# Expert stage of a hybrid diffusion step: rows gathered and added back by indirect DMA, weights in longer rows, an unrolled order

## The chip, the cores and the metric

One core of a Trainium2 chip runs the whole kernel. The metric is the device time of one execution in microseconds, the median of the runs shown. TensorE (PE) multiplies, VectorE (DVE) and ScalarE (ACT) work on tiles in SBUF and PSUM, GpSimd (POOL) does small work and issues some DMAs, SyncE (SP) issues the weight loads.

## The reference

One inference step of two layers on 128 context tokens and 256 latent tokens of 1024 channels. Layer 0 is differential attention and a dense SwiGLU, layer 1 a Fourier mixing and a top-2-of-8 expert SwiGLU; all is float32. The part that changes is the experts of layer 1:

```python
def moe_swiglu(h, w_router, w_gu_e, w_down_e):
    hf = h.reshape(-1, D_MODEL)
    probs = jax.nn.softmax((hf @ w_router).astype(F32), axis=-1)
    topv, topi = lax.top_k(probs, TOP_K)
    topv = topv / jnp.sum(topv, axis=-1, keepdims=True)
    gates = jnp.sum(jax.nn.one_hot(topi, N_EXPERTS) * topv[..., None], axis=1)
    out = jnp.zeros(hf.shape, F32)
    for e in range(N_EXPERTS):
        out = out + gates[:, e:e + 1] * swiglu(hf, w_gu_e[e], w_down_e[e])
    return out.reshape(shp)
# swiglu(h, w_gu, w_down): g, u = split(h @ w_gu); (silu(g) * u) @ w_down
# D_MODEL 1024, D_FF 2816, so w_gu_e[e] is 1024 x 5632 and w_down_e[e] 2816 x 1024
```

## The kernel before

All 384 tokens are handled together, as three tiles of 128. Every weight matrix is streamed from HBM in units of 1 MB (128 partitions x 2048 floats) into six slots `raw`. To multiply float32 accurately, each unit is split in two: ScalarE copies it to `ring_hi` in the type that TensorE multiplies fast (line 772 in the expert stage), VectorE subtracts to get the rest, `ring_lo` (line 1185). There are three such split slots (`RING`). The tokens are split in the same way. `mm3` (lines 1360 to 1364) does three matmuls for one product: high by high, low by high, high by low.

Each engine has its own program; semaphores order them. `unit_used` counts units that TensorE has finished, `hi_ready` and `lo_ready` the splits. SyncE loads unit m into a raw slot once unit m-6 has its low part; ScalarE splits a unit once its ring slot is used; both run two units ahead of TensorE (`AHEAD`).

The expert stage handles one expert at a time, with at most 128 of its tokens in the common path; a further block, which runs only where an expert has more than 128 tokens, stands behind it (its branch isn't taken with these inputs). A loop runs four times over a pair of experts. An expert has 33 units: 11 chunks of 256 gate and 256 up columns, each chunk two units (`gu`, half of the 1024 rows each, rows of 256 floats in HBM), and 11 `down` units of 256 rows. The order is gu, gu, then the down unit of the chunk before, so that TensorE has a down unit to do while ScalarE takes tanh and VectorE forms the hidden product `eh` (lines 1278 and 1281). `eh` is turned by TensorE (line 1694), split (lines 820 and 1268) and used by the down unit. Two PSUM banks take turns for gate/up, banks 4 and 5 collect the down product, 6 and 7 serve the rest.

The tokens of an expert are gathered by a product with a 0/1 matrix `sel`, which VectorE makes by comparing positions (line 1237): `gather_rows` (line 1645) multiplies `sel` by the split tokens `tok_hi` and `tok_lo`, 12 matmuls of 512 columns, `turn_gathered` (line 1654) turns the result into `xe`. After the expert its result `y`, split in two (lines 835 and 1285), is brought back to token order by the product with the turned selection (`bring_back`, line 1668, 12 matmuls of 512 columns), scaled by the gate and added to `acc` by VectorE (line 1261). These pieces are set by hand between the units of the next expert:

```python
COMBINE_AT = (8, 11, 14, 17, 18, 20)
NEXT_SEL_AT = 21
ROWS_AT = (24, 27)
TURN_AT = (26, 29)
SELT_AT = 30
```

Ahead of the stage stand the router's product, softmax and choice (lines 1192 to 1230), POOL's clearing of `acc` and others (line 562), and the first expert's gather. POOL works out the further blocks (`further_blocks`) while the first expert runs. In the last expert POOL multiplies `acc` by the residual gate `gbc` and adds it to `x` (lines 569 and 570). After the last expert come its own add-back, the final norm and the stores.

## Time and profile before

| | |
|---|---|
| median of 3 runs | 1582.09 us |
| the three runs | 1582.09, 1581.4, 1591.55 us |
| span of the profiled execution | 1587.8 us |
| instructions | 20380 |
| HBM read and written | 391.25 MB, 2.62 MB |
| PE, DVE, ACT, POOL busy | 94%, 71%, 53%, 12% of the span |

The profiled execution is one execution, with its own time: no time beside its span is given for it, and the span lies between the runs, 5.7 us above their median. All times inside the program (starts, waits) are counted from the start of that span. Matmuls overlap: the mean duration of one is longer than the step from one to the next, so the step is the price of a matmul in a row of them.

### The profile page before, as it was taken

How to read it: one execution, taken by the hardware profiler on the slowest of the kernel's cores; microseconds unless marked ns; L12 is line 12 of the kernel's file. 1: busy time of each engine (PE TensorE's matmuls, PEld its weight loads, DVE VectorE, ACT ScalarE, POOL GpSimd, SP SyncE). 2: the span in 40 equal slices, each digit the busy share in tenths (PEclk: the TensorE clock that was granted, in tenths of full speed). 3: DMA queues.
4: the chain of work that ended last, by engine and by line, in shares of the span. 5: the costliest groups of instructions: out<-in, count | busy, mean ns of one | idle time of the engine just before them, and what ended most of it. 6: DMA issues, size and time to landing. Idle time of an engine off the chain costs nothing.

```text
span 1587.8 us, 20380 instructions
## 1 busy us (share of the span) xinstructions
PE 1484.8 (94%) x6947; PEld 1169.5 (74%) x6947; DVE 1134.6 (71%) x1265; ACT 836.9 (53%) x935; POOL 196.7 (12%) x292
## 2 busy tenths in 40 slices
PE   5899988899999998988999999999999999999995
PEld 1776444699999984776877878878788787787873
DVE  1642764626455554456989989899899898898997
ACT  2431544523232224245667666676677767667764
POOL 4000332000000000006970000000000000000062
PEclk8999989999999998988999999999999999999997
DMA  9746896232433430224999999999999999999981
GB/s 346 286 162 249 340 380 240 93 107 89 150 126 113 134 105 0 85 75 160 345 317 354 334 317 349 326 336 348 314 344 338 321 355 324 310 341 319 358 297 70
DMA packets 258940, 395.32 MB, mean 249 GB/s; under 512 B 9905, under 2 KB 214882, under 8 KB 252690
## 3 DMA queue, kind: packets, MB, share of 16 engines
q1 hardware_dynamic: 256048, 386.44, 70.8%
q0 software_dynamic: 2144, 5.81, 1.2%
q10 hardware_dynamic: 642, 1.66, 0.3%
q8 instruction: 66, 1.08, 0.3%
q14 instruction: 40, 0.33, 0.1%
HBM read 391.25 MB, written 2.62 MB: 248 GB/s over the span
## 4 chain that ended last, share of the span: by engine, by line
PE 86%; DVE 7%; issue 2%; ACT 2%; DMA 2%; POOL 0%; DVEq 0%; SPq 0%; ACTq 0%
PE ps L1362 24%; PE ps L1364 24%; PE ps L1363 24%; PE ps L1374 2%; DVE ring_lo L1185 2%; DMA raw<-in_ada_w 2%; PE ps L1645 2%; PE ps L1668 1%; PE ps L1585 1%; PE ps L1694 1%; PE ps L1417 1%; PE ps L1496 1%; PE ps L1475 1%; PE ps L1399 1%; PE ps L1539 1%
## 5 line engine op out<-in xcount | busy, mean ns | idle before, releaser
L1185 DVE TENSOR_TENSOR ring_lo<-raw,ring_hi 128x2048 fp32r<-128x2048 f32 x266 | 612.0, 2311 | 66.3 <-ACT ring_hi L772 64.5
L772 ACT ACTIVATE ring_hi<-raw 128x2048 fp32r<-128x2048 f32 x266 | 508.1, 1912 | 53.3 <-PE ps L1364 53.3
L1362 PE MATMUL ps<-ring_hi,xe 128*128 128x512 f32 x704 | 285.2, 405 | 6.0 <-DVE ring_lo L1185 6.0
L1364 PE MATMUL ps<-ring_lo,xe 128*128 128x512 f32 x704 | 278.8, 396 | 0.0
L1363 PE MATMUL ps<-ring_hi,xe 128*128 128x512 f32 x704 | 278.5, 396 | 0.0
L903 DVE TENSOR_TENSOR ring_lo<-raw,ring_hi 128x2048 fp32r<-128x2048 f32 x53 | 120.4, 2288 | 144.0 <-ACT ring_hi L587 143.9
L587 ACT ACTIVATE ring_hi<-raw 128x2048 fp32r<-128x2048 f32 x53 | 101.2, 1913 | 180.2 <-PE ps L1364 154.2
L1362 PEld LDWEIGHTS ps<-ring_hi,xe 128*128 128x128 f32 x704 | 132.7, 188 | 36.9 <-issue 6.6
L1364 PEld LDWEIGHTS ps<-ring_lo,xe 128*128 128x128 f32 x704 | 132.5, 188 | 32.1
L1363 PEld LDWEIGHTS ps<-ring_hi,xe 128*128 128x128 f32 x704 | 132.9, 189 | 28.4
L1362 PE MATMUL ps<-ring_hi,eh_hi 128*128 128x512 f32 x352 | 139.9, 398 | 9.1 <-DVE eh_lo L1268 9.1
L1364 PE MATMUL ps<-ring_lo,eh_hi 128*128 128x512 f32 x352 | 139.1, 395 | 0.0
L1363 PE MATMUL ps<-ring_hi,eh_lo 128*128 128x512 f32 x352 | 139.1, 395 | 0.0
L1362 PE MATMUL ps<-h_hi,ring_hi 128*128 128x384 f32 x336 | 114.6, 341 | 2.0 <-DVE hb L1139 2.0
L1364 PE MATMUL ps<-h_lo,ring_hi 128*128 128x384 f32 x336 | 113.5, 338 | 0.0
L1363 PE MATMUL ps<-h_hi,ring_lo 128*128 128x384 f32 x336 | 113.5, 338 | 0.0
L1362 PE MATMUL ps<-ring_hi,h_hi 128*128 128x512 f32 x240 | 99.7, 416 | 5.5 <-DVE h_lo L967 5.5
L569 POOL TENSOR_TENSOR acc<-acc,gbc 128x512 f32<-128x512 f32 x6 | 13.9, 2313 | 693.8 <-DVE acc L1261 693.8
L1363 PE MATMUL ps<-ring_hi,h_lo 128*128 128x512 f32 x240 | 95.4, 398 | 0.0
L1364 PE MATMUL ps<-ring_lo,h_hi 128*128 128x512 f32 x240 | 95.3, 397 | 0.0
L820 ACT ACTIVATE eh_hi<-ps 128x256 fp32r<-128x256 f32 x88 | 33.8, 384 | 113.4 <-PE ps L1694 113.4
L1362 PEld LDWEIGHTS ps<-ring_hi,eh_hi 128*128 128x128 f32 x352 | 66.1, 188 | 27.4 <-issue 10.8
(250 smaller groups left out, 2143.0 us busy)
## 6 DMA issues: line engine op xcount, KB each, us to landing
raw<-in_w_gu_e SPq DMA_DIRECT2D x356, 512.0 KB, 5.1
raw<-in_w_down_e SPq DMA_DIRECT2D x88, 1024.0 KB, 7.0
raw<-in_ada_w SPq DMA_DIRECT2D x48, 1024.0 KB, 9.2
raw<-in_w_gu SPq DMA_DIRECT2D x44, 512.0 KB, 4.8
raw<-in_w_qkv SPq DMA_DIRECT2D x12, 1024.0 KB, 13.1
raw<-in_w_down SPq DMA_DIRECT2D x11, 1024.0 KB, 7.1
raw<-in_w_o SPq DMA_DIRECT2D x4, 1024.0 KB, 10.6
raw<-in_w_fourier SPq DMA_DIRECT2D x4, 1024.0 KB, 5.7
```

The costliest lines, as they stand in the source:

```text
L587: act.activation(ring_hi[:, s % RING, :], raw[:, u % RAW, :], ACT.Copy).then_inc(hi_ready, 1)
L772: act.activation(ring_hi[:, s % RING, :], raw[:, (MOE_U0 + m) % RAW, :], ACT.Copy).then_inc(hi_ready, 1)
L820: act.activation(eh_hi[:, par(j, c), :, :], ps[:, 2 + par(j, c), 0:256].rearrange("p (s n) -> p s n", s=2), ACT.Copy).then_inc(eh_hi_ready, 1)
L903: dve.tensor_tensor(ring_lo[:, s % RING, :], raw[:, u % RAW, :], ring_hi[:, s % RING, :].bitcast(F32), ALU.subtract).then_inc(lo_ready, 1)
L1185: dve.tensor_tensor(ring_lo[:, s % RING, :], raw[:, (MOE_U0 + m) % RAW, :], ring_hi[:, s % RING, :].bitcast(F32), ALU.subtract).then_inc(l ...
L1362: pe.matmul(out, l_hi, r_hi, start=first, stop=False)
L1363: pe.matmul(out, l_lo, r_hi, start=False, stop=False)
L1364: return pe.matmul(out, l_hi, r_lo, start=False, stop=last)
L1374: ins = pe.matmul(ps[32 * j:32 * j + 32, 7, :], cond[:, k, :], raw[:, u % RAW, j * HALF:(j + 1) * HALF], start=(k == 0), stop=(k == KC - 1))
L1399: ins = pe.transpose(ps[:, 2 * k + q // 4, (q % 4) * P:(q % 4 + 1) * P], xn[:, k, q * P:(q + 1) * P], ident[:])
L1417: pe.matmul(ps[:, bank, :], ident[:, row:row + 1].to_broadcast([P, P]), gates[:], start=True, stop=True).then_inc(gbc_ps, 1)
L1645: ins = pe.matmul(ps[:, 6, :], sel[:, b, k, :], part[:, k, half * HALF:(half + 1) * HALF], start=(r == 0 and k == 0), stop=(r == 1 and k = ...
```

## The change

- **Weights.** An expert's 2816 columns are three chunks of 1024, 1024 and 768. A gate/up unit is now 128 rows of the matrix with all of a chunk's gate and up columns (rows of 4 or 3 KB, eight units a chunk); a down unit is 256 rows, two neighbouring rows to a partition, 8 KB together. 35 units an expert, each one DMA. TensorE turns `eh` by every second column, to suit.
- **Order.** No loop. The units of all experts stand in one list: a chunk's eight gate/up units, then the down units of the chunk before, across experts too. The four PSUM banks 0 to 3 all serve one chunk.
- **Split buffers.** Four instead of three; splitting runs three units ahead.
- **Gather.** ScalarE stores the normed tokens to DRAM (`rows_dram`). A small product of the selection with token numbers gives a list of rows for each slot (`number_slots`), and POOL fetches an expert's rows by an indirect DMA into `xg`, which is turned into `xe`.
- **Add-back.** ScalarE scales `y` by the gate of each slot into `y_rows`, and POOL adds it to `acc_dram` in DRAM by an indirect DMA that accumulates. POOL clears `acc_dram` during the dense layer and loads it back in the last expert; VectorE then multiplies it by the gate `gbc` and adds it to `x` (`fold`). The last expert's result is still brought back by a product with the turned selection.

The diff, cut to its core:

```diff
-PAIRS = N_EXP // 2
 EXTRA = (2 * TOK) // (P + 1)
-PER_PAIR = 2 * NU
-AHEAD = 2
...
+CHUNKS = ((0, 1024), (1024, 1024), (2048, 768))
+NC = len(CHUNKS)
+RINGM = 4
+AHEAD = 3
+LAST = N_EXP - 1
+TURN_K = 2
+TURN_X_K = 5
...
+    out = []
+    for e in range(N_EXP):
+        out += gu(e, 0)
+        if e:
+            out += down(e - 1, NC - 1)
+        for c in range(1, NC):
+            out += gu(e, c) + down(e, c - 1)
+    return out + down(LAST, NC - 1)
...
+        def moe_source(m):
+            kind, e, c, n = MU[m]
+            if kind == "gu":
+                at, w = CHUNKS[c]
+                return t["w_gu_e_1"][e].rearrange("(k p) (u n) -> p k u n", p=P, u=2)[:, n, :, at:at + w]
+            at = CHUNKS[c][0] + 256 * n
+            return t["w_down_e_1"][e][at:at + 256, :].rearrange("(p s) n -> p (s n)", s=2)
...
-            with sp.Fori(0, PAIRS) as i:
-                for m in range(PER_PAIR):
-                    kind, c, kh = FFN_UNITS[m % NU]
-                    e = 2 * i + m // NU
-                    u = MOE_U0 + m
-                    sp.wait_ge(lo_ready, MOE0 + m - RAW + 1 + PER_PAIR * i)
-                    load(u % RAW, kind, c, kh, (t["w_gu_e_1"][e], t["w_down_e_1"][e]))
...
+            for m in range(NM):
+                slot = (MOE_U0 + m) % RAW
+                sp.wait_ge(lo_ready, MOE0 + m - RAW + 1)
+                dst = raw[:, slot, 0:width(m)]
+                if MU[m][0] == "gu":
+                    dst = dst.rearrange("p (u n) -> p u n", u=2)
+                sp.dma_start(dst, moe_source(m)).then_inc(raw_loaded[slot], 16)
...
+            pool.wait_ge(fflo_ready, 2 * FFC)
+            pool.memset(zeros[:], 0.0).then_inc(zero_ready, 1)
+            pool.wait_ge(zero_ready, 1)
+            for k in range(4):
+                pool.dma_start(acc_dram[k * P:(k + 1) * P, :], zeros[:]).then_inc(acc_zeroed, 16)
...
-            pool.wait_ge(tokT_ps, 2 * TILES)
-            for buf in (acc[:], y_hi[:].bitcast(F32), y_lo[:].bitcast(F32), selT[:, 1, :].bitcast(F32), gate_col[:]):
-                pool.memset(buf, 0.0).then_inc(zeroed, 1)
...
+            def bring_rows(e):
+                if e:
+                    pool.wait_ge(xe_ps, 2 * e)
+                pool.indirect_dma_start(xg[:], None, rows_dram, bass.IndirectOffsetOnAxis(ap=pick_to[:, e:e + 1], axis=0)
+                                        ).then_inc(xg_loaded, 16)
+            def send_rows(e):
+                pool.wait_ge(y_sb, e + 1)
+                if e:
+                    pool.wait_ge(y_sent, 16 * e)
+                pool.indirect_dma_start(acc_dram, bass.IndirectOffsetOnAxis(ap=send_to[:, e:e + 1], axis=0), y_rows[:],
+                                        None, compute_op=ALU.add).then_inc(y_sent, 16)
+            pool.wait_ge(idx_first, 1)
+            pool.wait_ge(rows_stored, 16 * TILES)
+            bring_rows(0)
+            pool.wait_ge(idx_ready, 1)
+            bring_rows(1)
             further_blocks()
-            pool.wait_ge(gbc_sb, 16)
-            pool.wait_ge(comb_sb, 6 * N_EXP)
-            for n in range(6):
-                k, cols = n // 2, slice((n % 2) * HALF, (n % 2 + 1) * HALF)
-                link(pool.tensor_tensor(acc[:, k, cols], acc[:, k, cols], gbc[:, COND[k], cols], ALU.mult))
-                pool.tensor_tensor(x[:, k, cols], x[:, k, cols], acc[:, k, cols], ALU.add).then_inc(x_folded, 1)
+            pool.wait_ge(acc_zeroed, 64)
+            for e in range(2, N_EXP):
+                bring_rows(e)
+                send_rows(e - 2)
+            send_rows(N_EXP - 2)
+            pool.wait_ge(y_sent, 16 * (N_EXP - 1))
+            pool.dma_start(acc[:], acc_dram[0:TOK, :].rearrange("(t p) n -> p t n", p=P)).then_inc(acc_loaded, 16)
...
+            def hi(m):
+                wait_moe_loaded(act, m)
+                w = width(m)
+                act.wait_ge(unit_used, MOE0 + max(0, m - RINGM + 1))
+                act.activation(ehi[m % RINGM][:, 0:w], raw[:, (MOE_U0 + m) % RAW, 0:w], ACT.Copy).then_inc(hi_ready, 1)
...
+            for k in range(TILES):
+                act.wait_ge(tokT_ps, 2 * k + 2)
+                act.activation(rows[:, k, :].rearrange("p (a n) -> p a n", a=2), ps[:, 2 * k:2 * k + 2, :],
+                               ACT.Copy).then_inc(rows_ready, 1)
+                act.wait_ge(rows_ready, k + 1)
+                act.dma_start(rows_dram[k * P:(k + 1) * P, :], rows[:, k, :]).then_inc(rows_stored, 16)
...
+            def tanh_gate(e, c):
+                w = CHUNKS[c][1]
+                act.wait_ge(unit_used, used_by("gu", e, c))
+                if NC * e + c:
+                    act.wait_ge(eh_ready, NC * e + c)
+                act.activation(et[:, 0:w].rearrange("p (a n) -> p a n", a=2), ps[:, 0:2, 0:w // 2], ACT.Tanh,
+                               scale=0.5).then_inc(et_ready, 1)
+            def keep_y(e):
+                act.wait_ge(unit_used, used_by("down", e, NC - 1))
+                if e < LAST:
+                    if e:
+                        act.wait_ge(y_sent, 16 * e)
+                    act.activation(y_rows[:].rearrange("p (a n) -> p a n", a=2), ps[:, 4:6, :], ACT.Copy,
+                                   scale=slot_gate[:, e:e + 1]).then_inc(y_sb, 1)
...
+            def select(e):
+                if e >= 2:
+                    dve.wait_ge(idx_ps, e - 1)
+                dst = selx[:] if e == LAST else sel[:, e % 2, :, :]
+                dve.tensor_tensor(dst, iota[:].unsqueeze(1).to_broadcast([P, TILES, P]),
+                                  posm[:, :, e:e + 1].to_broadcast([P, TILES, P]), ALU.is_equal).then_inc(sel_ready, 1)
...
+            def hidden(e, c):
+                n, w = NC * e + c, CHUNKS[c][1]
+                pair = lambda a: a[:, 0:w].rearrange("p (a n) -> p a n", a=2)
+                dve.wait_ge(et_ready, n + 1)
+                if n:
+                    dve.wait_ge(ehT_ps, 2 * n)
+                dve.scalar_tensor_tensor(pair(eh), pair(et), 1.0, ps[:, 0:2, 0:w // 2],
+                                         ALU.add, ALU.mult).then_inc(ea_ready, 1)
+                dve.wait_ge(ea_ready, n + 1)
+                dve.scalar_tensor_tensor(pair(eh), pair(eh), 0.5, ps[:, 2:4, 0:w // 2],
+                                         ALU.mult, ALU.mult).then_inc(eh_ready, 1)
...
+            def fold(n):
+                k, cols = n // 2, slice((n % 2) * HALF, (n % 2 + 1) * HALF)
+                link(dve.tensor_tensor(acc[:, k, cols], acc[:, k, cols], gbc[:, COND[k], cols], ALU.mult))
+                dve.tensor_tensor(x[:, k, cols], x[:, k, cols], acc[:, k, cols], ALU.add)
...
+                if kind == "gu" and (e, c) == (LAST, NC - 1) and n < 6:
+                    if n == 0:
+                        dve.wait_ge(acc_loaded, 16)
+                        dve.wait_ge(gbc_sb, 16)
+                    fold(n)
...
-            def gather_rows(e, b, half):
-                if half:
-                    pe.wait_ge(rows_sb, 2 * e + 1)
-                else:
-                    pe.wait_ge(sel_ready, e + 1)
-                for r, part in enumerate((tok_hi, tok_lo)):
-                    pe.wait_ge(tok_lo_ready if r else tok_hi_ready, 6)
-                    for k in range(TILES):
-                        ins = pe.matmul(ps[:, 6, :], sel[:, b, k, :], part[:, k, half * HALF:(half + 1) * HALF],
-                                        start=(r == 0 and k == 0), stop=(r == 1 and k == TILES - 1))
-                ins.then_inc(rows_ps, 1)
...
+            def number_slots(e):
+                pe.wait_ge(sel_ready, e + 1)
                 for k in range(TILES):
+                    lhs = selx[:, k, :] if e == LAST else sel[:, e % 2, k, :]
+                    ins = pe.matmul(ps[:, 6, 64 + 2 * e:66 + 2 * e], lhs, vals[:, k, e, :],
+                                    start=(k == 0), stop=(k == TILES - 1))
+                ins.then_inc(idx_ps, 1)
...
+            def turn_hidden(e, c):
+                for half in range(2):
+                    n = min(4, CHUNKS[c][1] // P - 4 * half)
+                    for q in range(n):
+                        g, r = (4 * half + q) // 2, q % 2
+                        rows_of = eh[:, 256 * g:256 * g + 256].rearrange("p (i s) -> p s i", s=2)[:, r, :]
+                        ins = pe.transpose(ps[:, 6 + half, q * P:(q + 1) * P], rows_of, ident[:])
+                    ins.then_inc(ehT_ps, 1)
...
-            with pe.Fori(0, PAIRS) as i:
...
+            for m in range(NM):
+                kind, e, c, n = MU[m]
+                before = (e, c - 1) if c else (e - 1, NC - 1)
+                if kind == "gu":
+                    if n == 0 and c == 0:
+                        pe.wait_ge(xe_lo_ready, 2 * e + 2)
+                    if n == 0 and NC * e + c:
+                        pe.wait_ge(eh_ready, NC * e + c)
+                    if n == TURN_K and NC * e + c:
+                        if c == 2 or (c == 1 and e):
+                            pe.wait_ge(eh_lo_ready, 2 * (NC * e + c - 1))
+                        elif c == 0:
                             pe.wait_ge(xe_lo_ready, 2 * e + 2)
+                        turn_hidden(*before)
+                    if n == TURN_X_K and c == NC - 1 and e < LAST:
+                        pe.wait_ge(eh_lo_ready, 2 * (NC * e + c))
+                        turn_gathered(e + 1, 6)
+                    pe.wait_ge(lo_ready, MOE0 + m + 1)
+                    hw = CHUNKS[c][1] // 2
+                    for b in range(4):
+                        w = slice(b * hw, (b + 1) * hw)
+                        ins = mm3(ps[:, b, 0:hw], xe[:, e % 2, 0, n, :], xe[:, e % 2, 1, n, :],
+                                  ehi[m % RINGM][:, w], elo[m % RINGM][:, w], n == 0, n == KC - 1)
```

## Rows read from the trace of the kernel before

**Rows 1.** Windows: stretch, busy us of each engine (instructions), clock, DMA share, GB/s.
```profile
690.00:730.00 40.00, 31.11 (x157) 24.40 (x156) 24.07 (x59) 20.90 (x41) 7.29 (x11) 0.74 0.16 53
1038.00:1141.00 103.00, 101.98 (x454) 81.82 (x454) 93.84 (x81) 72.45 (x62) 0.00 (x0) 1.00 0.99 336
```

**Rows 2.** Waits, 830 to 1520 us: who waited for whom, total, times, longest.
```profile
DVE ring_lo L1185 <- ACT ring_hi L772: 52.8, 94, 3.3
PE ps L1362 <- DVE eh_lo L1268: 7.2, 7, 1.0
PE ps L1362 <- DVE ring_lo L1185: 5.4, 3, 2.0
...
SPq L373 <- DVE ring_lo L1185: 362.1, 140, 4.4
```

**Rows 3.** PE's timeline: first and last of 29 matmuls of 512, 28 of 384.
```profile
938.24 0.39 PE L1363 MATMUL ps<-ring_hi,xe 128*128 128x512 f32 x1
...
944.77 0.39 PE L1364 MATMUL ps<-ring_lo,xe 128*128 128x512 f32 x1
...
419.77 0.34 PE L1364 MATMUL ps<-h_lo,ring_hi 128*128 128x384 f32 x1
...
424.45 0.34 PE L1364 MATMUL ps<-h_lo,ring_hi 128*128 128x384 f32 x1
```

**Rows 4.** Chain that ended last, 900 to 930 us: start, length, what (count).
```profile
912.09 0.44 PE ps L1654 x4
915.55 1.38 PE ps L1645 x6
```

**Rows 5.** PE's timeline: matmuls that it waited for, and the stage's first.
```profile
730.13 0.48 PE L1362 MATMUL ps<-ring_hi,xe 128*128 128x512 f32 x1
...
933.16 0.47 PE L1362 MATMUL ps<-ring_hi,eh_hi 128*128 128x512 f32 x1 [1.02 <-DVE eh_lo L1268]
...
1140.93 0.47 PE L1362 MATMUL ps<-ring_hi,eh_hi 128*128 128x512 f32 x1 [1.02 <-DVE eh_lo L1268]
...
1562.41 0.47 PE L1362 MATMUL ps<-ring_hi,eh_hi 128*128 128x512 f32 x1 [1.02 <-DVE eh_lo L1268]
```

**Rows 6.** Instruction groups, 830 to 1520 us: busy, mean ns, idle before.
```profile
L1185 DVE TENSOR_TENSOR ring_lo<-raw,ring_hi 128x2048 fp32r<-128x2048 f32 x220 | 501.7, 2289 | 54.5 <-ACT ring_hi L772 52.8
L772 ACT ACTIVATE ring_hi<-raw 128x2048 fp32r<-128x2048 f32 x220 | 420.2, 1912 | 44.0 <-PE ps L1364 44.0
L1285 DVE TENSOR_TENSOR y_lo<-ps,y_hi 128x1024 fp32r<-128x1024 f32 x7 | 8.6, 1225 | 0.0
L1243 DVE TENSOR_TENSOR xe<-ps,xe 128x512 fp32r<-128x512 f32 x12 | 8.2, 683 | 0.0
L835 ACT ACTIVATE y_hi<-ps 128x1024 fp32r<-128x1024 f32 x7 | 7.2, 1025 | 13.7 <-PE ps L1364 13.7
```

**Rows 7.** DMA, 830 to 1520 us; below it a window of an earlier stage.
```profile
DMA packets 174329, 230.58 MB, mean 334 GB/s; under 512 B 5849, under 2 KB 155591, under 8 KB 174279
...
200.00:210.00 10.00, 8.56 (x68) 4.85 (x64) 6.95 (x24) 4.19 (x15) 5.47 (x12) 1.00 1.01 421
```

**Rows 8.** Timeline: the routing on DVE and PE, and one POOL issue.
```profile
710.96 1.88 DVE L1219 TENSOR_TENSOR tok_lo<-ps,tok_hi 128x512 fp32r<-128x512 f32 x3
...
718.10 1.65 PE L1645 MATMUL ps<-tok_hi,sel 128*128 128x512 f32 x3 [3.09 <-DVE sel L1237]
...
30.75 0.56 POOL L524 DMA_DIRECT2D gbc<-in_cache_k  x1
```

**Rows 9.** DMA issues: name, queue, count, KB each, us to landing.
```profile
out_v_ctx<-v POOLq DMA_DIRECT2D x1, 512.0 KB, 5.2
...
out_y_prompt<-acc ACTq DMA_DIRECT2D x1, 512.0 KB, 3.4
```

**Rows 10.** One line alone by windows: L1185 beside no POOL work, then beside it.
```profile
830.00:930.00 100.00, 74.65 (x33) 1.00 0.99 336
1528.00:1555.00 27.00, 21.22 (x8) 1.00 0.72 237
```

## What the change will do to the time

> **What bounds the kernel now.** I began with the windows. An expert's stretch in the middle of the last stage shows TensorE busy 101.98 of 103 us at full clock, VectorE 93.84, ScalarE 72.45 and DMA engines at a share of 0.99 [rows 1]. Three of these could be the bound, so the waits come next. TensorE waited in 690 us only 7.2 us for VectorE's `eh_lo` and 5.4 us for `ring_lo`, and for no transfer; nor does a wait of ScalarE for a transfer stand there. VectorE waited 52.8 us for ScalarE, and SyncE's queue 362.1 us for a raw slot to come free [rows 2]. A queue that waits for slots is ahead, so the full DMA share is traffic in flight, not a limit. TensorE's own order is the bound. Its timeline gives the price of its work: 28 steps of a 512-column matmul between 938.24 and 944.77 are 0.233 us each, 27 steps of a 384-column one 0.173 us [rows 3]. The chain gives a transpose as 0.11 us (0.44 for four) and a gather half of six matmuls as 1.38 us, so 0.23 each, like the others [rows 4].
>
> Check on the stretch that changes. One expert has 33 units of 12 matmuls, 396 x 0.233 = 92.4 us; gather and add-back are 24 matmuls, 5.6 us; 33 transposes are 3.6 us: 101.6 us. Two experts took 1140.93 - 933.16 = 207.8 us [rows 5], 103.9 each; the 2.3 us left are the wait of 1.02 us ahead of each expert's last down unit [rows 5] and half of a wait of 1.8 us for `ring_lo` (5.4 us in three) where the loop turns [rows 2]. The stage runs from 730.13 to 1562.41 + 12 x 0.233 = 1565.2 [rows 5], 835.1 us; 22.6 us follow to the end of the span of 1587.8 us.
>
> **Part by part.** Matmul columns of the experts stay: per expert 16 gate/up units and 11 down units of 12 matmuls of 512 (324 x 0.233 = 75.6 us) and 8 units of 12 of 384 (96 x 0.173 = 16.6 us). What goes from TensorE is the gather, the add-back and the turning of the selection; 22 + 8 transposes stay, 3.3 us. Sum 95.5 us, 8.4 less than 103.9. Eight experts are 764 us; the last gathers for nobody, -0.9: **763 us**. The loop's turn and seven of the eight waits before the last down unit go with it, since the next expert's first units now stand between.
>
> Whether the others keep up decides if TensorE gets this. VectorE per expert: 27 `ring_lo` of 2048 and 8 of 1536 columns. A wide one takes 2.25 us back to back (74.65 us for 33 [rows 10]), the narrow one 1.7: 74.5 us. The products of a chunk run at 1024 or 768 columns; 1024 columns from PSUM cost 1.225 us and 512 cost 0.683 [rows 6], so four of 1.23 and two of 0.96 are 6.8. Splits of the turned hidden rows are five of 0.68 and one of 0.42, of the gathered rows two of 0.68: 5.2. Sum 86.5 us, some 90 with gaps, beside 95.5. ScalarE: 35 copies at 1.912 or 1.45 are 63, three tanh at 1.025 or less, the rest 5: 71 us [rows 6]. Both fit, VectorE closely.
>
> New waits, with what is queued behind them. (a) The four PSUM banks of gate/up are no longer double: the next chunk's first matmul waits for `eh`. After a chunk's last matmul come tanh 1.0, two products 2.45 and gaps, 4.0 us; three or four down units of 2.8 us lie between, so it costs nothing, except after expert 0's first chunk, where no down unit exists: **+4.0 us**. (b) On VectorE `hidden` stands ahead of the next `ring_lo`. ScalarE splits unit m once unit m-4 is used, so when a chunk ends VectorE is still on the third unit ahead for 1.5 us; then 2.5 for the products, 2.25 for the next split: 6.3 us. The three units split ahead hold TensorE 8.4 us. Cost nothing, margin 2.1 us; in the narrow chunk VectorE's work (five narrow and three wide splits, four of 0.68 for hidden and gathered rows, gaps: 18.7 us) is as long as TensorE's (8 x 2.08 + 16 transposes: 18.4), and the margin falls to some 1.3. (c) The fold of the accumulated rows moves from POOL to VectorE, into the last expert's narrow chunk: 12 instructions of 0.68 and gaps, 8.7 us. From the first of these units to the split of the last hidden rows VectorE then has 5 x 1.7 + 7 x 2.25 of splits, 8.7 of fold, 1.9 of products, 2.5 of hidden rows, and it starts 1.5 late: 39 us, beside 8 narrow units, 14 transposes and 4 down units, 16.6 + 1.5 + 11.2 = 29.3, on TensorE: **+9.7 us**. Bounds 3 (VectorE enters ahead) and 14. (d) Gather and add-back by POOL. The trace shows no indirect transfer. A plain POOL issue takes 0.56 us [rows 8] and a 512 KB store of it 5.2 us to land [rows 9]. The gathered buffer is refilled right after it was turned and is next wanted 95 us later; an add-back has as long. The tightest is the last: sent after expert 6's last down unit, then 1.5 MB come back before the fold, with some 33 us of cover for two such transfers and a larger one, some 20 us by these rows. Bounds 0 to +10; I take 0.
>
> POOL's reads beside a split are not free: beside POOL's fold a `ring_lo` took 21.22/8 = 2.65 us, alone 2.26 [rows 10]. Fifteen indirect issues cost at most some 6 us of VectorE, spread out, within its margin: 0.
>
> Before the stage. Three splits are made ahead instead of two (+2.25 on VectorE ahead of the routing) and some small constants (+0.8), while three `tok_lo` (1.88 us [rows 8]) go: slot numbers about 1 us later than the 718.10 at which the gather starts now. Then comes a chain that is new: last rows stored by ScalarE's queue (3.4 to 5.2 us to land [rows 9]; behind its three issues stand only the gate copies, wanted later) by about 722.5, gather issued and landed (0.56 + 5.2) by 728.3, eight transposes and the split of their halves, 4 us: first unit at 732.5 beside 730.13, +2.4. TensorE idles in it; the clock over 690 to 730 us was 0.74 in the mean [rows 1], between the levels of 2.4 GHz (1.0) and 1.2 GHz (0.5), and I add 2 us for units at the lower one: **+4.4 us**, bounds -2 (both land in 3.4) and +12 (both take twice 5.2). The clearing of the DRAM accumulator (one memset, four issues of 0.56 us on POOL [rows 8], some 4 us) lies ahead of POOL's third norm, but the dense layer's last down unit, 36 matmuls of 0.233 or 8.4 us, stands between: nothing. Should it miss that cover, 4 us.
>
> Sum: 763 + 4.0 + 9.7 = 776.7 against 835.1, -58.4; +4.4; **-54 us** on a span of 1587.8. That span lies 5.7 us above the median of the three runs, 1582.09, and inside their range; I take the difference off the median: **1528 us**.
>
> **Rivals.** *The weight stream.* The stage must bring the experts' 8 x 3 x 1024 x 2816 x 4 bytes = 276.8 MB, less some 9 loaded before it, and 12 MB of rows: 280 MB in 777 us, 360 GB/s. Before, it moved 334 GB/s at a share of 0.99 [rows 7]; were that its limit, 280 MB would take 838 us and the time would be 1582 + 7 = 1589, no gain, and the change would not do what it says. Against it: SyncE's 362 us of waiting for slots, and 421 GB/s where rows of 8 KB are loaded [rows 7], by which 665 us would do. Of its 174,329 packets 155,591 were below 2 KB, the gate/up rows of 1 KB nearly all of them; those rows are now 3 and 4 KB. Between these ends I lean on the 421. A core's limit of 358 GB/s would make it 280/0.358 = 782 us, 5 more than the sum: 1533. The Trainium skill (HBM Reference, "Specifications (TRN2)") gives 358 GB/s as a core's share of its memory; the 421 of this trace contradicts that as a limit for one core alone.
>
> *The slower side: splits run dry at chunk ends.* Should VectorE enter each chunk end with only one unit split instead of three, TensorE would wait 6.3 - 2.8 = 3.5 us at 23 chunk ends, 80 us: 1608. It decides from the point where the cover falls below 6.3 - 54/23 = 3.95 us, 1.4 units. For it: VectorE's 90 of 95.5 us, the 8-unit narrow chunk in which it gains nothing. Against it: the fourth buffer, and that it regains 0.5 us per wide unit.
>
> *The strided turn.* The hidden rows are now transposed from every second element, which no row here shows. If such a transpose cost twice the 0.11 us, 176 of them add 19 us: 1547; at the same price nothing. The Trainium skill (Advanced Engine Details and Errata, "SBUF Cachelines") asks for two hits on each 16-byte line; every second float makes just two, so by it the price stays. No run here shows it yet, and it lowers this rival's chance.
>
> **How the numbers follow.** Forecast and its near variants 0.72; the strided turn 0.07; the weight stream as the limit 0.10, half of it near 1533 to 1550, half at 1589; chunk ends dry 0.06 at 1608; something better, such as a shorter chain before the stage, 0.05. Range: below, 1528 less 6 (before the stage) and 7 (fold) gives 1515; above, 8 more before the stage, 4 of the fold and a microsecond at 20 chunk ends give 1560. A measurement of this kernel, whose three runs differ by 10 us, tells 1%, 16 us, from no change. Faster by more (below 1566): 0.72 + 0.07 + 0.05 + 0.05 = 0.89; within: 0.05; slower: 0.06.
>
> **What would show it.** Right: experts repeating every 95 to 97 us on TensorE, matmuls 0.233 us apart, no group with gather or selection, one wait of some 4 us after the first chunk and one or more of some 10 us in all in the last expert; first expert matmul near 732. Wrong: TensorE waiting for `eh` or `ring_lo` at every chunk end (rival two), ScalarE's `ring_hi` waiting for transfers (rival one), transposes of `eh` above 0.11 us apart, a first matmul after 745, or VectorE held before the fold by the returning rows.

## The result and the profile after

The changed kernel took 1539.22 us in the median of four runs (1537.82 to 1540.71) beside 1584.69 us for the kernel before: ratio 0.9699, 95% interval 0.9669 to 0.9729. Run again later with five runs beside nine of before (e11 below) it took 1536.03 beside 1589.95: 0.967, 0.9654 to 0.9686. (The ratios here and below stand on record with the runs; they are not the quotients of the medians.) It is faster by 3%; forecast were 1528 us and 1515 to 1560.

The profiled execution took 1538.5 us, its span is 1536.6. The top of its page (busy time and instructions of each engine, the DMA's packets):

```profile
PE 1436.4 (93%) x6951; PEld 1167.2 (76%) x6951; DVE 1063.2 (69%) x1037; ACT 817.8 (53%) x814; POOL 187.0 (12%) x296
...
DMA packets 115479, 406.07 MB, mean 264 GB/s; under 512 B 7649, under 2 KB 30354, under 8 KB 97986
```

The windows of two experts (columns as in [rows 1]) and the waits from 830 to 1520 us, as in [rows 2]:

```profile
859.00:955.00 96.00, 96.00 (x453) 81.32 (x453) 86.27 (x50) 71.36 (x49) 3.29 (x3) 1.00 0.98 374
955.00:1050.00 95.00, 95.00 (x449) 80.55 (x448) 85.27 (x50) 70.42 (x47) 3.20 (x2) 1.00 0.98 374
```

```profile
DVE ring_lo L1280 <- ACT ring_hi L861: 49.4, 99, 1.0
...
POOL acc L649 <- DMA acc_dram<-y_rows,send_to: 10.5, 1, 10.5
...
SPq L462 <- DVE ring_lo L1280: 407.8, 179, 4.0
SPq L462 <- DVE ring_lo_more L1280: 131.9, 60, 4.0
```

TensorE is busy without a gap, no transfer appears among what ScalarE or TensorE waited for, and SyncE's queue waits for slots more than before: the same bound, with less work in it. The line that takes an expert's result from PSUM gives the period (first and last start):

```profile
L915 ACT ACTIVATE y_rows<-ps,slot_gate x7: 1114/1117/1120, 858.1 to 1431.1; 128x1024 f32<-128x1024 f32 x7
```

(1431.1 - 858.1) / 6 = 95.5 us an expert, as forecast; before it was 103.9 [rows 5]. What surrounds the experts is seen on PE's timeline (start, length, line, count, and in brackets the wait with its releaser):

```profile
691.16 1.09 PE L1502 MATMUL ps<-ident,xn 128*128 128x128 f32 x8 [0.93 <-ACT xn L694]
...
718.34 6.54 PE L1744 MATMUL ps<-vals,sel 128*128 128x2 f32 x36
...
726.02 4.94 PE L1520 MATMUL ps<-gates,ident 128*128 128x512 f32 x6
...
731.12 1.04 PE L1754 MATMUL ps<-ident,xg 128*128 128x128 f32 x8
734.10 0.47 PE L1465 MATMUL ps<-ring_hi,xe 128*128 128x512 f32 x1 [1.94 <-DVE xe L1337]
...
760.68 0.53 PE L1465 MATMUL ps<-ring_hi,xe 128*128 128x512 f32 x1 [4.03 <-DVE eh L1359]
761.02 0.62 PE L1466 MATMUL ps<-ring_hi,xe 128*128 128x512 f32 x1
761.44 0.63 PE L1467 MATMUL ps<-ring_lo,xe 128*128 128x512 f32 x1
...
1485.70 0.47 PE L1465 MATMUL ps<-ring_hi,eh_hi 128*128 128x512 f32 x1 [1.27 <-DVE ring_lo L1280]
...
1502.93 0.79 PE L1465 MATMUL ps<-ring_hi,eh_hi 128*128 128x512 f32 x1 [3.76 <-DVE eh_lo L1344]
1503.52 0.63 PE L1466 MATMUL ps<-ring_hi,eh_lo 128*128 128x512 f32 x1
...
1513.68 0.39 PE L1467 MATMUL ps<-ring_lo_more,eh_hi 128*128 128x512 f32 x1
1516.44 0.50 PE L1772 MATMUL ps<-y_hi,selT 128*128 128x512 f32 x1 [2.37 <-DVE y_lo L1393]
```

Three rows of the kernel before that were not shown, the turns behind the last norm ahead of the routing, the three gate spreads ahead of the first unit and the first add-back of the last expert:

```profile
693.84 1.09 PE L1399 MATMUL ps<-ident,xn 128*128 128x128 f32 x8 [0.93 <-ACT xn L605]
...
726.97 2.74 PE L1417 MATMUL ps<-gates,ident 128*128 128x512 f32 x6
...
1567.89 0.50 PE L1668 MATMUL ps<-y_hi,selT 128*128 128x512 f32 x1 [2.45 <-DVE y_lo L1285]
```

These marks split the difference of the spans, 1587.8 - 1536.6 = 51.2 us. Up to the norm's turns 693.84 became 691.16: -2.7, which is within chance (in the twelve runs below, which leave that part alone, the turns start between 689.11 and 695.14). From there to the first expert matmul 36.29 became 42.94: +6.7, forecast +4.4. From there to the end of the last down unit 835.2 became 779.8 (1513.68 + 0.23 - 734.10): -55.3, forecast -58.4. The tail, 22.5 us and 22.7, stayed.

These are TensorE's waits in the stage (four short ones are left out of the rows): 4.03 us after expert 0's first chunk, then none for 718 us, then six in the last expert, 6.7 us together. Behind the two long ones the matmuls are 0.43 us apart instead of 0.233. The windows say why (span, PE, PEld, DVE, ACT, POOL, granted clock, DMA share, GB/s); the first lies ahead of the stage:

```profile
718.00:731.00 13.00, 13.00 (x55) 10.12 (x55) 3.40 (x11) 1.19 (x2) 1.11 (x1) 0.61 0.16 52
...
756.70:760.70 4.00, 0.02 (x1) 0.02 (x1) 3.97 (x4) 2.81 (x2) 3.43 (x9) 1.00 1.03 389
760.70:764.30 3.60, 3.60 (x9) 2.88 (x10) 2.15 (x1) 0.00 (x0) 3.12 (x7) 0.54 0.71 241
...
1503.00:1508.50 5.50, 5.50 (x13) 4.33 (x14) 0.00 (x0) 0.00 (x0) 0.00 (x0) 0.50 0.02 4
```

After the idle 4.03 and 3.76 us the granted clock is at its lower level (0.54 and 0.50 in these windows; 0.5 is 1.2 GHz): nine matmuls at 0.425 instead of 0.233 are 1.7 us more, thirteen at the end 2.5.

### The profile page after: what moved, and what is told of

Same layout as the page of the kernel before. It is cut to its first block, busy times and chain, and to the rows that moved or that the text cites. A ratio compares the mean times of both kernels' runs of the same rounds, so it can differ in the third digit from the quotient of the medians.

```text
span 1536.6 us, 17394 instructions
## 1 busy us (share of the span) xinstructions
PE 1436.4 (93%) x6951; PEld 1167.2 (76%) x6951; DVE 1063.2 (69%) x1037; ACT 817.8 (53%) x814; POOL 187.0 (12%) x296
## 4 chain that ended last, share of the span: by engine, by line
PE 87%; DVE 6%; ACT 2%; DMA 2%; issue 1%; POOL 0%; DVEq 0%; SPq 0%; ACTq 0%
PE ps L1465 25%; PE ps L1467 25%; PE ps L1466 25%; PE ps L1477 2%; DVE ring_lo L1280 2%; PE ps L1688 1%; DMA raw<-in_w_qkv 1%; PE ps L1763 1%; PE ps L1520 1%; DMA raw<-in_ada_w 1%; PE ps L1578 1%; PE ps L1599 1%; PE ps L1642 1%; PE ps L1744 1%; ACT h L709 1%
## 5 line engine op out<-in xcount | busy, mean ns | idle before, releaser
L1280 DVE TENSOR_TENSOR ring_lo<-raw,ring_hi 128x2048 fp32r<-128x2048 f32 (+1 forms) x210 | 451.8, 2167 | 66.4 <-ACT ring_hi L861 64.9
L861 ACT ACTIVATE ring_hi<-raw 128x2048 fp32r<-128x2048 f32 (+1 forms) x210 | 381.9, 1821 | 142.8 <-PE ps L1467 142.1
L1465 PE MATMUL ps<-ring_hi,xe 128*128 128x512 f32 (+1 forms) x576 | 219.1, 380 | 6.6 <-DVE eh L1359 4.0
L998 DVE TENSOR_TENSOR ring_lo<-raw,ring_hi 128x2048 fp32r<-128x2048 f32 x53 | 120.4, 2289 | 144.2 <-ACT ring_hi L676 144.2
L1467 PE MATMUL ps<-ring_lo,xe 128*128 128x512 f32 (+1 forms) x576 | 217.0, 377 | 0.0
L1466 PE MATMUL ps<-ring_hi,xe 128*128 128x512 f32 (+1 forms) x576 | 216.8, 376 | 0.0
L676 ACT ACTIVATE ring_hi<-raw 128x2048 fp32r<-128x2048 f32 x53 | 101.1, 1912 | 180.8 <-PE ps L1467 154.8
L1280 DVE TENSOR_TENSOR ring_lo_more<-raw,ring_hi_more 128x2048 fp32r<-128x2048 f32 (+1 forms) x70 | 151.7, 2168 | 18.2 <-ACT ring_hi_more L861 17.8
L861 ACT ACTIVATE ring_hi_more<-raw 128x2048 fp32r<-128x2048 f32 (+1 forms) x70 | 127.4, 1821 | 42.4 <-PE ps L1467 42.2
L1465 PEld LDWEIGHTS ps<-ring_hi,xe 128*128 128x128 f32 x576 | 108.7, 189 | 24.6 <-DVE eh L1359 4.5
L1466 PEld LDWEIGHTS ps<-ring_hi,xe 128*128 128x128 f32 x576 | 108.4, 188 | 17.2
L1477 PE MATMUL ps<-raw,cond 128*32 128x512 f32 x384 | 58.5, 702 | 18.0 <-DMA raw<-in_ada_w 15.2
```

The source lines that it names most:

```text
L676: act.activation(ring_hi[:, s % RING, :], raw[:, u % RAW, :], ACT.Copy).then_inc(hi_ready, 1)
L861: act.activation(ehi[m % RINGM][:, 0:w], raw[:, (MOE_U0 + m) % RAW, 0:w], ACT.Copy).then_inc(hi_ready, 1)
L998: dve.tensor_tensor(ring_lo[:, s % RING, :], raw[:, u % RAW, :], ring_hi[:, s % RING, :].bitcast(F32), ALU.subtract).then_inc(lo_ready, 1)
L1280: dve.tensor_tensor(elo[m % RINGM][:, 0:w], raw[:, (MOE_U0 + m) % RAW, 0:w], ehi[m % RINGM][:, 0:w].bitcast(F32), ALU.subtract).then_inc(l ...
L1465: pe.matmul(out, l_hi, r_hi, start=first, stop=False)
L1466: pe.matmul(out, l_lo, r_hi, start=False, stop=False)
```

## The experiments

My theory: TensorE's order is the bound, and the gain is the work taken out of it (24 matmuls and 3 transposes an expert) and the waits of the loop, less the wait after the first chunk, the fold and the longer way to the first unit. The rivals were the weight stream, the split buffers and the strided turn. "Stage" is from the first expert matmul to the first add-back of the last expert, 782.34 us in the changed kernel; the way to the first unit is from the norm's turns, 42.94 us there. Both are read from PE's timeline. In e11, the same kernel again, they are 782.23 and 42.63, while the medians of that kernel differ by 3 us. One thing moves the stage by 1 to 1.5 us by chance: how many matmuls behind the wait of the last turn run at the lower clock (thirteen in the changed kernel, eight in e1, e3 and e4, none in e7 and e9). All edits start from the changed kernel.

**e1, short rows.**

```diff
-                sp.dma_start(dst, moe_source(m)).then_inc(raw_loaded[slot], 16)
+                    for at in range(0, CHUNKS[MU[m][2]][1], 256):
+                        sp.dma_start(dst[:, :, at:at + 256],
+                                     moe_source(m)[:, :, at:at + 256]).then_inc(raw_loaded[slot], 16)
...
```

> The gate/up units of the experts come in rows of 1 KB again (three or four transfers a unit where there was one), as in the kernel before; all else is as changed. My theory: the changed stage is TensorE's own order and the weights are off the path, so the time stays, 1537 to 1545 us, SyncE still waits for slots to come free, and TensorE has no new waits. Rival, the row length made the gain: at 1 KB the stream ends at the 334 GB/s of before, 280 MB take 838 us instead of 782, and the time is some 1595 us, with ScalarE's splits waiting for transfers in every expert.

Measured 1552.72 us (1551.41 to 1556.94), ratio 0.9781 (0.9764 to 0.9798); stage 795.93, +13.6. Both expectations miss. ScalarE now waits for transfers (830 to 1400 us), and the DMA view of 900 to 1000 us shows 40 slices at full share, more than half of them at 343 to 354 GB/s:

```profile
ACT ring_hi L865 <- DMA raw<-in_w_gu_e: 72.7, 72, 2.4
...
ACT ring_hi_more L865 <- DMA raw<-in_w_gu_e: 26.9, 25, 2.6
```

```profile
DMA  9999999999999999999999999999999999999999
GB/s 421 429 413 388 371 348 352 348 348 348 347 353 351 379 423 419 390 350 347 349 347 349 349 349 354 227 363 413 426 423 415 363 349 349 348 345 343 352 394 426
```

The slices near 420 are those of down units with rows of 8 KB. So gate/up units in pieces of 256 KB with rows of 1 KB have a limit of their own, 348 GB/s here, above the 334 that the kernel before wanted [rows 7] and below the 374 that the changed one wants. One transfer in long rows instead of four in short ones is worth 13.6 us. That it is worth this only because TensorE became faster is inferred from SyncE's waits for slots before [rows 2]; no run gave the kernel before long rows. The rest of the gain stands without them.

**e12, two transfers a unit** (gate columns and up columns, rows of 4 and 3 KB) asks if the number of transfers was to blame.

```diff
-                sp.dma_start(dst, moe_source(m)).then_inc(raw_loaded[slot], 16)
+                    for a in range(2):
+                        sp.dma_start(dst[:, a, :], moe_source(m)[:, a, :]).then_inc(raw_loaded[slot], 16)
...
```

> A gate/up unit comes as two transfers, the gate columns and the up columns, each over all 128 partitions, with rows of 4 and 3 KB as in the changed kernel: the number of transfers of the kernel before with the long rows. In e1 the transfers of 1 KB rows ran at a flat 348 GB/s and those of 8 KB rows at 420, so I hold the row length for its price: 1535 to 1541 us here, and ScalarE waits for no transfer. If the number of transfers has a price, a third to a half of what e1 lost comes: 1541 to 1547 us.

Measured 1541.86 us (1540.6 to 1543.14), 0.9703 (0.9687 to 0.9719). The median lies just above the expected 1541, in the rival's range, but the stage is 1518.73 - 736.39 = 782.34 us, the changed kernel's to the hundredth, and neither ScalarE nor TensorE waits for a transfer; the profiled execution is longer by 2.1 us, ahead of the norm's turns. Two transfers cost nothing in it. The kernel before, also with two transfers a unit but rows of 1 KB, moved 336 GB/s at a DMA share of 0.99 [rows 1]; here it is 374 at 0.98. This speaks for the length of the rows as the cause in e1. That three or four transfers cost nothing either, with rows as long, was to be seen in the next run, and wasn't, so this part of the cause is not shown.

**e8, four transfers cut by partitions.**

```diff
-                sp.dma_start(dst, moe_source(m)).then_inc(raw_loaded[slot], 16)
+                    parts = (0, 32, 64, 96, P) if MU[m][2] < 2 else (0, 48, 96, P)
+                    for a, b in zip(parts, parts[1:]):
+                        sp.dma_start(dst[a:b], moe_source(m)[a:b]).then_inc(raw_loaded[slot], 16)
...
```

> The gate/up units come in as many transfers as in e1 (four a unit, three in the narrow chunk), but cut by partitions, so that their rows stay 4 and 3 KB. It tells apart what made e1 some 13 us slower. If it was the length of the rows (packets of 1 KB cost the DMA engines more), this run stays at the time of the changed kernel, 1536 to 1542 us, and ScalarE waits for no transfer. If it was the number of transfers (SyncE's issues, or completions), it is as slow as e1, 1549 to 1556.

Measured 1882.05 us in the median of three runs (1878.0 to 1901.24; a fourth took 1921.43), 1.1888 (1.1819 to 1.1957), outside both expectations: it shows another effect and leaves its own question open. Its stream from 900 to 1000 us:

```profile
GB/s 247 269 270 259 261 413 423 378 195 193 200 210 226 224 229 231 237 236 240 239 283 346 419 416 318 239 223 228 236 239 239 249 243 244 244 243 254 254 252 244
```

The down units, over all partitions, still pass at 413 to 423; the quarters move at 193 to 283, most at some 240, at a full DMA share. The Trainium skill ("SBUF — State Buffer", "Door 1: The DMA port swizzle") gives a reason: bandwidth depends on how many of 16 memory ports a transfer's partitions reach, and 32 neighbouring partitions reach eight. Its peak of 436 GB/s halved is 218 as an estimate. The 240 is near it, but no run here separates this from other reasons.

**e2, three split buffers.**

```diff
-RINGM = 4
-AHEAD = 3
+RINGM = 3
+AHEAD = 2
```

> Three split buffers instead of four, two units split ahead instead of three. My theory: at a chunk's end VectorE is away from the splits for some 6.3 us and four buffers cover 8.4; three cover 5.6, so TensorE waits about 0.7 us at each of some 22 chunk ends, a little more behind the narrow chunk: 1550 to 1565 us. Rival A, the fourth buffer does nothing: 1539. Rival B, the buffers alone made the change work: waits of 3 us and more at every chunk end, 1605 to 1620 us.

Measured 1565.35 us (1563.3 to 1565.43), 0.9847 (0.9832 to 0.9862), the upper edge of the theory; stage 807.53, +25.2.

```profile
PEld ps L1465 <- DVE ring_lo L1280: 16.1, 17, 1.0
PE ps L1465 <- DVE ring_lo L1280: 10.3, 22, 0.6
```

The waits for `ring_lo` are back (the rows are from 830 to 1400 us), each of 1 us or less, and the period is 98.65 us. The margin was counted right in kind: with one unit less of cover the splits run dry, at 25.2 / 23 = 1.1 us a chunk end where the arithmetic gave 0.7. The fourth buffer carries half of the gain, as a condition.

**e3, the turn without a stride.**

```diff
-            return t["w_down_e_1"][e][at:at + 256, :].rearrange("(p s) n -> p (s n)", s=2)
+            return t["w_down_e_1"][e][at:at + 256, :].rearrange("(s p) n -> p s n", s=2)
...
-                        rows_of = eh[:, 256 * g:256 * g + 256].rearrange("p (i s) -> p s i", s=2)[:, r, :]
+                        rows_of = eh[:, 256 * g + P * r:256 * g + P * r + P]
```

> The hidden rows are turned from 128 neighbouring columns instead of every second one; for that a down unit holds two rows of 4 KB in a partition instead of one of 8 KB. My theory: the stride cost TensorE nothing on its path, 1537 to 1541 us; the weight loads of the turn go from 209 back to some 140 ns without a change of the time. Rival, each strided turn costs TensorE a second 0.11 us: 176 of them are 19 us, and the time falls to 1520. If rows of 4 KB stream worse than rows of 8 KB, the time rises above 1545 and ScalarE waits for transfers.

Measured 1535.13 us (1531.57 to 1538.94), 0.9659 (0.9641 to 0.9676); stage 779.79, -2.55. The turn's weight loads and matmuls (ns min/median/max), first in the changed kernel, then here:

```profile
L1763 PEld LDWEIGHTS ps<-ident,eh x176: 194/209/214, 767.7 to 1498.8; 128*128 128x128 f32 x176
L1763 PE MATMUL ps<-ident,eh x176: 270/283/288, 767.9 to 1498.9; 128*128 128x128 f32 x176
```

```profile
L1765 PEld LDWEIGHTS ps<-ident,eh x176: 137/141/143, 770.0 to 1499.4; 128*128 128x128 f32 x176
L1765 PE MATMUL ps<-ident,eh x176: 270/272/273, 770.2 to 1499.6; 128*128 128x128 f32 x176
```

On PE's timeline eight turns take 0.87 us with the stride (863.46 to 864.33) and 0.79 without: 0.01 us each, 1.8 us in 176, so the period falls to 95.27. Up to the end of the last turn's wait the stage is 1.6 us shorter; the other 1.0 is the clock behind that wait. The rival's 19 us are refuted; "nothing" was a little too little. Rows of 4 KB do no harm.

**e4, the fold late.**

```diff
-                if kind == "gu" and (e, c) == (LAST, NC - 1) and n < 6:
...
+                if kind == "down" and (e, c) == (LAST, NC - 1):
+                    if n == 0:
+                        low_eh(e, c)
+                        dve.wait_ge(acc_loaded, 16)
+                        dve.wait_ge(gbc_sb, 16)
+                    fold(2 * n)
+                    fold(2 * n + 1)
```

> The fold of the accumulated rows goes from the last expert's narrow chunk to its last three down units, behind the last split that VectorE makes, where VectorE stood idle for 12.28 us. My theory: the six waits of TensorE in the last expert, 6.7 us together, were the price of the fold, and 8.2 us of fold fit into the idle time: 1532 to 1534 us, and at most one wait of 1 us is left in the last expert. Rival, these waits belong to the narrow chunk itself and only showed there for other reasons (no gathered rows, no next units): 1538 to 1540. The fold's end sets the tail if it takes over 12 us: then 1540 or more.

Measured 1531.52 us (1528.94 to 1535.36), 0.9644 (0.9628 to 0.966); stage 775.63, -6.71. One wait is left in the last expert, longer than the 1 us expected:

```profile
1496.16 0.50 PE L1465 MATMUL ps<-ring_hi,eh_hi 128*128 128x512 f32 x1 [2.28 <-DVE eh_lo L1344]
...
1508.68 0.50 PE L1772 MATMUL ps<-y_hi,selT 128*128 128x512 f32 x1 [2.37 <-DVE y_lo L1393]
```

Its 2.28 us are the last turn's own, for which no unit is left as cover; eight matmuls behind it run at the lower clock, 0.43 us each. The wait for `y_lo` has not grown. The fold cost 6.7 us where it stood, and nothing in VectorE's idle time.

**e5, TensorE's work back.**

```diff
+                        pe.wait_ge(lo_ready, MOE0 + m + 1)
+                        for r in range(8):
+                            pe.matmul(ps[:, 6, :], xe[:, e % 2, 0, n, :], ehi[m % RINGM][:, 0:HALF],
+                                      start=(r == 0), stop=(r == 7))
                         turn_hidden(*before)
```

> TensorE gets back as many matmuls as the change took from it: eight of 512 columns ahead of each turn of hidden rows, 23 times (the last turn excepted), 184 in all; what they compute is overwritten and enters no output. My theory: TensorE's order is the bound, so all of them stand on the path, 184 x 0.233 = 42.9 us: 1580 to 1584 us. Rival, the gain came from the loop's end, the long rows and the deeper buffers, and TensorE has room: under 1550 us.

Measured 1580.83 us (1578.55 to 1583.95), 0.9954 (0.9936 to 0.9971); stage 823.16, +40.8.

```profile
L915 ACT ACTIVATE y_rows<-ps,slot_gate x7: 1117/1119/1122, 865.3 to 1471.7; 128x1024 f32<-128x1024 f32 x7
```

The period is 101.07 us, 5.6 more, and 24 x 0.233 = 5.6: every matmul stands on the path, and from 830 to 1520 us TensorE waits for nothing. With them the change is worth 0.5%. The rival, room on TensorE, is refuted.

**e6, less work on TensorE.**

```diff
-                        ins = mm3(ps[:, b, 0:hw], xe[:, e % 2, 0, n, :], xe[:, e % 2, 1, n, :],
+                        ins = mm2(ps[:, b, 0:hw], xe[:, e % 2, 0, n, :], xe[:, e % 2, 1, n, :],
...
```

`mm2` leaves out the last of the three matmuls of `mm3`, here and in the down units.

> The experts' products leave out the third of the three matmuls (high part of the rows by low part of the weights), so TensorE's work in the stage falls by a third, to some 65 us an expert, and everything else, loads and splits included, stays. It asks what the next bound is. My theory: VectorE, 86.3 us busy an expert and some 90 with its gaps; the stage shortens by 4 to 8 us an expert, 1475 to 1510 us, VectorE is busy at 95% or more, and the loads go at 395 to 420 GB/s. Rival, the weight stream is already at its limit at 374 GB/s and a DMA share of 0.98: no gain, 1535 to 1540 us, and ScalarE's splits wait for transfers.

Measured 1487.73 us (1485.38 to 1488.97), 0.9371 (0.9342 to 0.9401); the period is 89.8 us. One window, and what ScalarE waited for from 830 to 1400 us:

```profile
859.00:949.00 90.00, 73.14 (x309) 55.27 (x308) 84.31 (x50) 69.08 (x47) 11.26 (x10) 0.96 1.03 402
```

```profile
ACT ring_hi L861 <- DMA raw<-in_w_gu_e: 51.9, 73, 2.0
ACT ring_hi L861 <- DMA raw<-in_w_down_e: 29.2, 43, 2.0
```

With a third of the matmuls gone only 5.7 us an expert are gained. The stream passes 402 GB/s, so 374 was no limit; VectorE is busy 94% of the time, and ScalarE waits for transfers as well. The two next bounds lie together, 6 us below TensorE's, and this run does not part them.

**e7, three moves:** the fold late, as in e4; all turn-backs of the rows ahead of the mask; three gate spreads into the wait after the first chunk. The cut shows the third.

```diff
...
+                    if n == 0 and (e, c) == (0, 1):
+                        for j in range(1, 4):
+                            spread_gate(3, j, GATE_BANKS[j])
                     if n == 0 and NC * e + c:
                         pe.wait_ge(eh_ready, NC * e + c)
...
```

> The changed kernel with three moves: the fold late, as in e4; all six turn-backs of the rows ahead of the wait for the selection mask, so that the last rows are stored some 4 us earlier; three of the four gate spreads from the way to the first expert unit into the wait after expert 0's first chunk. My theory: fold 6 us less; the first unit no longer waits for the gates (4.94 us at the lower clock) but for the gathered rows, which come 2 us earlier, so 3 to 5 us less; the spreads hide in the wait of 4.03 us: 1527 to 1531 us. Rival, the way to the first unit is set by the numbering of the slots and the landing of the gather alone, which do not move: 1532 to 1534, as with the late fold alone. If the spreads are not hidden, 2 to 3 us come back after the first chunk.

Measured 1529.68 us (1527.36 to 1533.22), 0.9633 (0.9605 to 0.9661).

```profile
734.46 0.76 PE L1467 MATMUL ps<-ring_hi,xe 128*128 128x512 f32 x1 [1.61 <-DVE xe L1339]
735.02 0.63 PE L1468 MATMUL ps<-ring_hi,xe 128*128 128x512 f32 x1
...
759.58 2.74 PE L1522 MATMUL ps<-gates,ident 128*128 128x512 f32 x6
763.76 0.50 PE L1467 MATMUL ps<-ring_hi,xe 128*128 128x512 f32 x1 [1.45 <-DVE eh L1361]
764.10 0.39 PE L1468 MATMUL ps<-ring_hi,xe 128*128 128x512 f32 x1
```

The way to the first unit is 39.92 us, 3.0 less: the spreads did stand on it. They hide behind the first chunk, and the matmuls there are 0.23 apart at once. But the first 14 matmuls of the stage now run at the lower clock, 0.43 us each, which gives 2.7 us back, so the stage gains 0.4 on e4 (775.27). Against e4, whose way is 42.58, that is 3.0 us by the marks. But half of it is the clock behind the last turn's wait of 2.28 us, which fell in e4 and not here: that stretch takes 12.52 us there and 10.99 here. The moves are worth the other 1.5; the medians differ by 1.8.

**e9 and e10:** the three moves with e3's straight turn; in e10 the turn-backs stay where the changed kernel has them.

> The three moves of e7 and the straight turn of e3 together. The stage of e7 took 775.27 us from its first matmul to the first of the last add-back, and the straight turn took 2.55 us off that stretch in e3: some 772.7 here, and 1524 to 1529 us in all. If the 2.55 us were chance, 775 and 1527 to 1531.

> As e9, but the last turn-backs of the rows stay behind the selection mask's sums, where the changed kernel has them. In e7 TensorE had less to do ahead of the first unit and its first 14 matmuls came 0.43 us apart instead of 0.233, 2.7 us lost. If the turn-backs held the clock up, the first unit here comes some 2 us later than in e9 after the third norm's turns, but its matmuls are 0.233 us apart at once: the same time as e9 within 1 us. If the clock falls here too, because TensorE waits for the gathered rows, it is 2 to 3 us slower than e9.

Measured e9 1527.77 us (1526.22 to 1532.52), 0.9621 (0.9605 to 0.9637), stage 772.19; e10 1529.46 us (1525.57 to 1531.1), 0.9617 (0.9603 to 0.9631), stage 773.92. The straight turn's gain holds: of the 3.1 us from 775.27 to 772.19, 1.4 come from the start, where seven matmuls fewer than in e7 take 0.43 us, and 1.7 are left for the turn. In e10 the first unit comes 39.06 us after the norm's turns, sooner than e9's 39.94, and its first matmuls are at 0.43 as well: neither expectation for the turn-backs is right, their place makes 0.9 us on the way. That e10's stage is 1.7 us longer is not their doing: behind the last turn's wait of 2.3 us the granted clock is 0.50 in e10 and 1.00 in e9, which makes 1.4 of it.

**e11, the changed kernel again.**

> The changed kernel itself once more, on the same chip as the three above: 1535 to 1541 us, and a tighter ratio to the kernel before, which I expect between 0.966 and 0.971.

Measured 1536.03 us (1534.23 to 1540.49), 0.967 (0.9654 to 0.9686), stage 782.23, way to the first unit 42.63. On the same chip e9 is 8.3 us faster.

## Why the prediction was right, and where it was off

The sign, the bound and the mechanism held, and the size within the range. By its steps:

**TensorE's order** was the bound and its price list right: 95.5 us an expert by sum and by trace, and e5 returns 5.6 us of period for 5.6 us of matmuls. (In the check on the kernel before, the two waits named make 1.9 of the 2.3 us; 0.4 us an expert stayed unexplained.) **VectorE** was forecast at 86.5 us an expert and is busy 86.27 of 96; ScalarE 71 and 71.36.

**(a)** 4.0 us after the first chunk: the wait is 4.03, but the step left out the clock. The wait drops it, and 1.7 us follow. e7 shows both: work put into the wait hides, and the next matmuls stay at 0.23.

**(b)** No cost at the chunk ends, margin 2.1 us: no wait stands in 718 us, and e2, which takes 2.8 us of cover away, brings 3.2 us an expert. This also settles the slower rival: its mechanism is real, but with one buffer less it costs 25 us, not the 80 at which it was priced.

**(c)** The fold, +9.7 (3 to 14): the last expert has 6.7 us of waits, and 2.5 us at the lower clock behind them. By e4 6.7 of this is the fold; 2.3 is the last turn, which the step had in its sum of VectorE's work but not as a wait of its own.

**(d)** Gather and add-back by POOL, 0: no engine but POOL itself waits for them in the stage. The add-back lands in 12.1 us and the 1.5 MB in 12.0, longer than I estimated, within the cover: POOL sends for the rows at 1445.09, they are back by some 1458, and the fold starts at 1468.75.

**Before the stage,** +4.4: measured +6.65. The chain that I followed was forecast well. Counted from the norm's turns, which came 2.7 us earlier, the rows were to be stored after 28.7 us and were after 28.6 (719.74), and gathered after 34.5 and were after some 33 (about 724). But it is not what the first unit waited for. What failed is that TensorE's own queue ahead of the turn was not counted: the numbering of the other slots and three gate spreads keep it until 731.1, with the rows there 7 us before. e7 takes the spreads away and gets 3.0 us, e10 3.9. The lower clock came, but not on the first unit, whose matmuls are 0.233 apart: the granted clock is 0.61 from 718 to 731 us, and the three spreads take 4.94 us there beside 2.74 before, 2.2 us more. That the 2 us set aside for it have this size is luck, since they were meant for the units; on these it comes in e7.

**The stage** is then 779.8 us beside 776.7: 1.7 and 2.5 of clock too little, 3.0 too much for the waits of the last expert, and 1.9 that no run assigns. That the first three nearly cancel is luck.

**From span to median.** -54 on the span against -51.2. The difference was taken off a median of three runs, 1582.09; with more runs the kernel before has medians of 1589.2 to 1590.0. This, more than any step, is why 1528 was low: in e11's set the difference is 1589.95 - 1536.03 = 53.9 us.

**The weight stream:** refuted as a limit of the changed kernel (e6 at 402 GB/s), but not as idle as the argument had it. The 421 on which I leaned was that of long rows; with rows of 1 KB in four transfers a unit 348 is the end (e1), and 13.6 us would have been lost. **The strided turn** costs a tenth of its 0.11 us, not as much again. By the Trainium skill (Advanced Engine Details and Errata, "SBUF Cachelines") two hits on a line are enough, so it would be free. The step nearly agrees, 0.109 beside 0.099 us; the weight load itself does not, 209 ns beside 141.

Left open: whether the length of the rows alone made e1 slower, why quarters by partitions are so slow (e8), whether VectorE or the stream is next (e6), and what in the routing holds the first unit now. In e7 it is still TensorE's own queue: the numbering of the slots runs there from 718.47 to 730.26, at a granted clock of 0.50, and no wait stands between it and the turn.

## What to carry to other kernels

Where an engine's own order is the bound, price each instruction by its step in a row of them, and look at what else stands in that engine's queue ahead of a new chain: the chain that was added is rarely alone. A cover of buffers should be checked against the longest absence of the splitting engine, since one buffer less cost half of the gain here. Work with slack belongs where its engine idles, not where its data first arrive: moving the fold by some 30 us gave 6.7 us for nothing.

## What the runs showed of the hardware that was not expected

- A wait of TensorE costs more than itself: after 4.03 and 3.76 us the granted clock was 0.54 and 0.50, with nine and thirteen matmuls at 0.43 us. After one of 2.3 us it fell in e4 and e10, and stayed at 1.00 in e7 and e9.
- Units of 1 MB that come as four transfers in rows of 1 KB flatten at 348 GB/s (e1); as one transfer in rows of 4 or 8 KB, or as two in rows of 4 KB, they pass at some 400 to 430, at the same full DMA share.
- A unit cut into quarters of 32 partitions moves at some 240 GB/s with rows of 4 KB, and the kernel takes 1882 us (e8).
- An indirect gather of 128 rows of 4 KB lands in 8.2 us (median of eight, the first in about 4), the accumulating add-back in 12.1.
